# An expert loop whose rounded table moves both token parts at once, in 512 columns, with the two halves of the bank added afterwards

## The reference

```python
idx = i1 * PEER_NKEYS + i2
g = jax.nn.softmax(best_s.astype(jnp.float32), axis=-1).astype(xb.dtype)
act = jax.nn.gelu(jnp.einsum('tpkd,td->tpk', u_tab[idx], xb), approximate=False)
return jnp.einsum('tpk,tpkd->td', g * act, v_tab[idx])
```

## Time and profile before

| | |
|---|---|
| median of 3 runs | 1550.94 us (1549.51 to 1551.19) |
| the profiled execution's own time | 1550.3 us |
| its span in the profile | 1548.6 us |
| PE busy | 1527.4 us (99%) |
| VectorE busy | 1195.0 us (77%) |
| ScalarE busy | 775.7 us (50%) |
| read from HBM, written | 274.60 MB, 17.83 MB |

### The profile page before, as it was taken

How to read it: one execution, slowest core, us unless ns; L and a number is a source line. 1 busy time by engine, 2 the same in 40 slices (tenths; PEclk the granted TensorE clock), 3 DMA queues, 4 the chain that set the end, 5 groups by cost and what they waited for, 6 DMA issues and landing times.

```text
span 1548.6 us, 27605 instructions
## 1 busy us (share of the span) xinstructions
PE 1527.4 (99%) x10124; PEld 1368.6 (88%) x10124; DVE 1195.0 (77%) x2050; ACT 775.7 (50%) x1110; POOL 60.4 (4%) x108
## 2 busy tenths in 40 slices
PE   8999999999999999999999999999999999999998
PEld 7678897988999887989999999999998888888886
DVE  7997645788736968757689999988875777777776
ACT  5237544565535563425444655645545455445553
POOL 2002000100000034000000000000000000000000
PEclk9999999999999999999999999999999999999999
DMA  7364668455533230516277777555558877777772
GB/s 290 128 246 156 233 232 324 163 191 191 187 112 111 87 109 2 203 55 243 87 224 220 231 226 221 172 167 154 158 156 287 256 242 240 239 243 242 239 241 76
DMA packets 95941, 293.64 MB, mean 190 GB/s; under 512 B 10480, under 2 KB 45424, under 8 KB 82928
## 3 DMA queue, kind: packets, MB, share of 16 engines
q1 hardware_dynamic: 95712, 292.21, 58.0%
q10 hardware_dynamic: 144, 0.26, 0.0%
HBM read 274.60 MB, written 17.83 MB: 189 GB/s over the span
## 4 chain that ended last, share of the span: by engine, by line
PE 86%; DVE 10%; DMA 2%; ACT 1%; issue 1%; SPq 0%; POOL 0%; DVEq 0%; POOLq 0%; ACTq 0%
PE ps L489 85%; DVE big L1557 1%; DVE split_ring L2180 1%; DVE big L1582 1%; DMA ring<-in_peer_u 1%; DMA ring<-in_peer_v 0%; DVE big L2040 0%; DMA ring<-kept_acts 0%; DVE big L1464 0%; DVE big L2228 0%; DVE big L2232 0%; DVE big L2230 0%; DMA ring<-in_w_gv 0%; DMA x<-in_x 0%; DVE big L1540 0%
## 5 line engine op out<-in xcount | busy, mean ns | idle before, releaser
L489 PE MATMUL ps<-split_hh,split_ring 128*128 128x256 f32 (+1 forms) x3648 | 522.1, 291 | 1.1 <-DVE split_ring L2180 1.0
L489 PEld LDWEIGHTS ps<-split_hh,split_ring 128*128 128x128 f32 x3648 | 460.0, 191 | 12.4 <-DVE split_ring L2180 1.9
L489 PE MATMUL ps<-split_ring 128*128 128x512 f32 (+1 forms) x1456 | 368.6, 382 | 1.5 <-DVE split_ring L2180 1.2
L489 PEld LDWEIGHTS ps<-split_ring 128*128 128x128 f32 x1456 | 266.2, 188 | 55.1 <-DVE split_ring L2180 2.1
L2180 DVE TENSOR_TENSOR split_ring<-ring,split_ring 128x1024 fp32r<-128x1024 f32 x192 | 233.7, 1220 | 48.9 <-ACT split_ring L2795 45.7
L2795 ACT ACTIVATE split_ring<-ring 128x1024 fp32r<-128x1024 f32 x128 | 135.2, 1057 | 82.5 <-DMA ring<-in_peer_u 82.5
L2284 DVE TENSOR_TENSOR ring<-ring,big 128x256 f32<-128x256 f32 x128 | 81.3, 636 | 76.7 <-PE ps L489 72.9
L489 PE MATMUL ps<-split_ffn_h,split_ffn_w 128*128 128x256 f32 (+1 forms) x720 | 123.8, 334 | 0.0
L489 PEld LDWEIGHTS ps<-split_ffn_h,split_ffn_w 128*128 128x128 f32 x720 | 109.3, 190 | 14.2
L489 PE MATMUL ps<-split_hid_high,split_ffn_w 128*128 128x258 f32 (+1 forms) x736 | 112.0, 284 | 0.2
L2802 ACT ACTIVATE split_ring<-ring 128x1024 fp32r<-128x1024 f32 x64 | 68.0, 1062 | 87.3 <-PE ps L489 81.5
(11 more groups left out here) (353 smaller groups left out, 2036.4 us busy)
## 6 DMA issues: line engine op xcount, KB each, us to landing
ring<-in_peer_u SPq DMA_DIRECT2D x128, 512.0 KB, 3.9
ring<-in_peer_v SPq DMA_DIRECT2D x64, 512.0 KB, 4.2
hh<-in_peer_v SPq DMA_DIRECT2D x64, 512.0 KB, 4.1
ring<-in_w_mod SPq DMA_DIRECT2D x24, 1024.0 KB, 6.1
ring<-in_ffn_in SPq DMA_DIRECT2D x22, 1024.0 KB, 5.0
ring<-kept_acts SPq DMA_DIRECT2D x128, 128.0 KB, 3.7
ring<-in_ffn_out SPq DMA_DIRECT2D x11, 1024.0 KB, 4.9
ring<-in_w_out SPq DMA_DIRECT2D x8, 1024.0 KB, 8.9
```

What stands on the lines that cost most here:

```text
L489: return nc.tensor.matmul(out, lhsT, rhs, start=start, stop=stop, skip_group_check=True)
```

## The change

For blocks 76 to 123 (`WIDE`) the two products that share the rounded table as stationary operand become one. The moving operand is `split["hh"][:, :, k, :]`, both token parts side by side, 512 columns in two runs; the left half of the bank then holds high x high, the right half high x low. The product low x high still has 256 columns and goes to the left half. So a block has 8 matmuls with 512 columns and 8 with 256.

The two halves must be added. ScalarE copies the right half to SBUF (`right_half`, in the place of `ones` and 128 columns more), VectorE adds it to the left half in the bank (`add_halves`, at the head of the low part three blocks on), and ScalarE applies Gelu to the sum. Between its copy and its Gelu ScalarE rounds the tile three blocks ahead, which before came after the Gelu. The eight last blocks are written out instead of a loop of two rounds. After the last block VectorE fills `ones` again. Some flags of the second loop's tiles share the semaphores of the first loop's (`tile_landed`), with counts to match.

```diff
+WIDE = (G_AT, 124)
...
-        ones = sb("ones", [P, P])
+        right_half = sb("ones_or_right_half", [P, T])
+        ones = right_half[:, 0:P]
...
         def activation_bank(q):
-            return ps[:, plan.bank["psc", 1, q % 2], 0:T]
+            return ps[:, plan.bank["psc", 1, q % 2], :]
...
+            def wide_activations(c, q):
+
+                pe.wait_ge(u_split, c + 1)
+                pe.wait_ge(s_read, c - 1)
+                bank = activation_bank(q)
+                for k in range(KD):
+                    mm(bank, u_high[q][:, k * P:(k + 1) * P], split["hh"][:, :, k, :], k == 0, False)
+                for k in range(KD):
+                    last = mm(bank[:, 0:T], u_low[:, q, k * P:(k + 1) * P], h_high[:, k, :], False, k == KD - 1)
+                last.then_inc(s_made, 1)
...
                 for c in range(u_before(g), u_before(g + 1)):
+                    wide_activations(c, c % 4)
+            for c in range(U_AT, NE):
+                if c < WIDE[1]:
+                    wide_activations(c, c % 4)
+                else:
                     activations(c, c % 4)
-            with pe.Fori(U_AT // 4, NE // 4) as i:
-                for q in range(4):
-                    activations(4 * i + q, q)
...
+            def add_halves(c):
+
+                dve.wait_ge(flag("right_copied"), c - WIDE[0] + 1)
+                left = activation_bank(c)[:, 0:T]
+                v.tensor_tensor(left, left, right_half, ALU.add).then_inc(flag("halves_added"), 1)
+
             def next_u(count=1):
 
                 for _ in range(count):
+                    if WIDE[0] <= u_at[0] - 3 < WIDE[1]:
+                        add_halves(u_at[0] - 3)
                     low_of("u", u_at[0], u_at[0] % 4)
                     u_at[0] += 1
...
             next_u(NE - u_at[0])
+            s.wait("halves_added", WIDE[1] - WIDE[0])
+            link(v.memset(ones, 1.0))
...
+            def wide_activate(c):
+
+                q, n = c % 4, c - WIDE[0]
+                act.wait_ge(s_made, c + 1)
+                if n:
+                    act.wait_ge(flag("halves_added"), n)
+                a_(right_half, activation_bank(q)[:, T:], ACT.Copy).then_inc(flag("right_copied"), 1)
+                high_u(c + 3, (q + 3) % 4, (c + 3) // 4)
+                act.wait_ge(flag("halves_added"), n + 1)
+                act.wait_ge(flag(f"act_out{q % 2}"), 16 * (c // 2))
+                a_(acts[q % 2], activation_bank(q)[:, 0:T], ACT.Gelu).then_inc(s_read, 1)
...
                 for c in range(u_before(g), u_before(g + 1)):
-                    activate(c, c % 4, c // 4)
-            activated(U_AT // 4, NE // 4 - 1)
+                    wide_activate(c)
+            for c in range(U_AT, WIDE[1]):
+                wide_activate(c)
```

## The result

| | before | after |
|---|---|---|
| median of six runs | 1549.8 us | 1560.04 us (1559.37 to 1561.0) |
| ratio, 95% interval | | 1.0066 (1.0057 to 1.0076) |
| profiled execution, span | 1550.3, 1548.6 | 1559.37, 1557.6 |
| PE busy | 1527.4 us | 1524.8 us |
| matmul and weight load records | 10124 each | 9740 each |

The change made the kernel 10.2 us slower, 0.66%. The forecast was 1559.0, from 8.1 us of loss. PE has 384 matmuls fewer and is busy for 2.6 us less, and still ends 9 us later: most of the loss is time in which it waits.

A forecast was written before the change was run, and what follows sets the result against it. PE, busy 99% of the span, was taken to bound the kernel; start +4.0, blocks 80 to 119 -4.8, six places +8.5, end +0.4 gave +8.1 us, 1559.0 as median; range 1551.5 to 1565.

The forecast's parts named there:

- The repeating place: Before groups 9, 12, 17, 20, 25, 28: PE waits 1.20 or 1.63 us as adds queue behind one-hots; +8.5 us.
- The start: Groups 2 to 4: VectorE enters with a backlog, delaying the first adds, so group 4 begins 4.0 us late.
- PE's gain: Blocks 76 to 123: wide matmuls at 0.225 us against 0.120 for narrow ones save 0.12 us a block.
- The end: Blocks 120 to 123: ScalarE's rounding waits for a landing ahead of Gelu; +0.4 us, from -0.2 to +0.9.
- The adds come in time: Rival: VectorE reaches each add within the block PE has in hand, only the gain is left; 1545.2 us, chance 0.13.
- The delay is paid once: Rival: after the late start a stagger makes the six places cost nothing; 1550.5 us, chance 0.13.
- The wide matmul gains nothing: Rival: 512 columns in two runs cost 0.24 us, as two narrow matmuls; 1562.6 us, chance 0.12.

The follow-up runs named there:

- the later start: The changed kernel with the change only for blocks 84 to 123, blocks 76 to 83 as before; 1555.67 us, ratio 1.0034.
- the run without adds: The changed kernel without copy and add, Gelu reading the left half at once, part of the result left out; 1546.05 us, ratio 0.9972.
- the narrow halves: The changed kernel with each wide matmul cut into two of 256 columns, copy, add and order kept; 1562.75 us, ratio 1.0077.
- both mended: The changed kernel with adds ahead of the next group's one-hots and the change for blocks 77 to 123; 1547.58 us, ratio 0.9982.
- the add between the sets: The changed kernel for blocks 77 to 123, with the add between a group's two one-hot sets; 1550.84 us, ratio 1.0000.
- the kernels with the adds moved: The changed kernel with adds ahead of the one-hots, for blocks 77 to 123 (1547.58 us) and for blocks 77 to 119 (1546.41 us).
- the moved add: The changed kernel with only a group's first add moved ahead of its one-hots on VectorE; 1549.89 us, ratio 0.9996.

## Why the prediction was right

**The repeating place**, the core of it, came out step by step. Forecast: PE waits before groups 9, 12, 17, 20, 25 and 28, and before no block. The trace has these six and only these behind the start. The chain was put at 5.73 us after the block's end; measured from 1027.99 to 1033.82 it is 5.83. Against the 4.59 us of a group without a wait each costs 1.24 us. Forecast were 1.20 for three of them and 1.63 for the others. The 0.43 more was wrong: VectorE was not late there but early, idle for 0.27 us before 1029.08. The step that failed took PE's gain (3 x 0.12) and the add's 0.40 for VectorE's delay; the adds take 0.34 apart (1032.34 to the next operation at 1032.68), PE came only 0.24 earlier, and the landing that starts this sequence came some 0.5 us sooner than in before. Six places: 7.4 us instead of 8.5.

**The start** was forecast at 4.0 us until group 4 and is 3.88, with group 2 at 1.84 (forecast) and 1.92. The working counts two wide blocks as 5.56 us where its own price gives 5.52; nothing hangs on it, since VectorE's order sets the 4.0. The run with the later start shows the start by itself: 4.4 us are back, the half speed behind it included.

**PE's gain** was mis-sized. The forecast took 0.120 and 0.225 us from two other stretches and got 0.12 a block; the run without adds measures 0.084, the trace 0.08. In after the first wide matmul behind an expert-weight group starts 0.31 us before the next (0.20 for a narrow one), and the others of the block stand 0.231 apart: 1018.04, 1018.27, 1018.50 and so on to 1019.66. By the rule of the Trainium skill that was weighed there (TensorE: Matmul & The Clock Gate, section "Wait — 56ns, not 53.3ns?"), a fixed cost of about 2.5 ns a matmul, the estimate would be 0.02. The measurement lies between that and the forecast, nearer to the forecast.

**The half-speed stretch** was in no term. It is 1.66 us in the profiled execution and the largest single thing missing. But such stretches are not the change's alone. Traces have them also in code that is the same in all these kernels: before at 42 us (as the narrow halves and "both mended"), the later start and the add between the sets at 621 us. The windows of before, and then of after, at the first of these places:

```profile
40.00:42.00 2.00, 2.00 (x15) 1.54 (x13) 2.00 (x6) 2.00 (x6) 0.00 (x0) 1.00 0.22 90
42.00:44.00 2.00, 2.00 (x3) 0.76 (x3) 1.96 (x6) 2.00 (x3) 0.00 (x0) 0.52 0.00 0
...
40.00:42.00 2.00, 2.00 (x14) 1.34 (x12) 2.00 (x6) 2.00 (x5) 0.00 (x0) 1.00 0.04 16
42.00:44.00 2.00, 2.00 (x6) 0.94 (x5) 1.96 (x6) 2.00 (x3) 0.00 (x0) 1.00 0.00 0
```

PE was busy for all of the 2 us ahead in both, and the clock fell only in before. The other five executions of after have a mean granted clock of 0.997 or 0.998 against 0.999 in the profiled one, but executions of before range from 0.997 to 1.000 as well. So how much half speed the change's waits add to its median is not shown.

**The end** was put at +0.4 us. From group 31 to the 37th matmul of the second loop after is 0.5 us quicker than before. The landings did bind, at the low end of what was feared: ScalarE's rounding waits for one and Gelu stands behind it,

```profile
1178.15 1.06 ACT L2828 ACTIVATE split_ring<-ring 128x1024 fp32r<-128x1024 f32 x1 [0.87 <-DMA ring<-in_peer_u]
1179.12 0.37 ACT L2863 ACTIVATE acts<-ps 128x256 f32<-128x256 f32 x1
```

and blocks 122 to 124, counted from their first matmuls, take 8.77 us in after (1176.70 to 1185.47) against 8.47 with the wide matmuls alone (1164.21 to 1172.68). The Gelu above is that of block 121, whose bank block 123 needs; it begins at 1179.63. These 0.3 us eat more than half of the 0.5 that six wide blocks gain here. What makes the end quicker lies in no term: from the first matmul of the second loop to the 37th, where PE waits for VectorE's low parts, it takes 9.50 us in after and 9.93 in before. These waits differ from trace to trace (0 to 0.97 us before the first of them), so the -0.5 may be chance as well.

By terms, forecast and trace: start +4.0 and +3.9; half speed 0 and +1.6; groups 5 to 31 +3.7 (8.5 less 4.8 gained) and +5.1 (six places of 1.30, the 0.06 being lost in the group behind each wait, less some 2.7 gained); end +0.4 and -0.5. Together that is 8.1 and 10.1 us; the medians say 10.2. The mechanism carried the forecast, but that the number came so close is in part luck: a smaller gain and an unseen half-speed stretch were partly offset by shorter waits and an end that came out quicker.

**The rivals.** "The adds come in time" is refuted by the eight waits; the kernels with the adds moved come near to it (1547.58 and 1546.41 against its 1545.2). "The delay is paid once" is refuted by the six equal waits. "The wide matmul gains nothing" is refuted by the run without adds; its 1562.6, the price of the same kernel with no gain, was nearly met by the halves without the wide matmul at 1562.75, in part by chance, since no half speed followed its waits at the start, as it did in after.

## What to carry to other kernels

A short operation put on another engine costs what stands before it in that engine's queue, and here this was work that waits for the very engine it is to release: look at what the new step queues behind, what that waits for, and who is queued behind the receiver of the step. Busy shares (VectorE 77%) would have passed the change; the order decided, and moving one 0.42 us add ahead of work that had time turned 10 us of loss into none. Read the granted clock of both traces before a stretch at half speed is put down to the change. When an engine works through a backlog, the first uses of a new hand-over meet it at its worst, and starting one block later can be worth more than the blocks left out.

## What the runs showed of the hardware

- Three profiles had a wait of 1.90 to 2.07 us on PE with a stretch at the lower granted clock behind it (after, the moved add, the add in the middle), each costing 1.66 to 1.69 us; after's first wait of 1.90 us, and the two of 1.75 us with narrow matmuls, had none. So the same gap may or may not bring it, and a gap can cost nearly twice its length. The clock also fell at 42 us in three of the nine traces and at 621 us in two, in code that the others ran at 1.00.
- A wide matmul whose 512 moving columns lie in two runs of 256 stood 0.231 us from the next, against 0.225 for one run in the second loop; the first one behind other work took 0.31.
- A VectorE add with both its input and its output in a PSUM bank took 0.42 to 0.43 us for 256 columns, as with one PSUM operand, and 0.34 until the next operation.
